# One ring of weight pieces across stage ends, and the first top-16 pass inside the key-score stages, in a hybrid encoder step

## The chip, the cores and the metric

One core of a Trainium2 chip runs the whole program. The metric is the device time of an execution in microseconds.

## What is computed

One inference step of a two-layer encoder, for 256 prompt tokens and 128 sample tokens (8 streams of 16), so three tiles of 128 tokens, width 1024, f32. Each layer has a mixer (layer 0: RWKV-7; layer 1: differential attention) and an expert mixer:

```python
q = (xr @ w_query).reshape(n, PEER_HEADS, 2, PEER_DHALF)
s = jnp.einsum('nhcd,ckd->nhck', q, sub_keys)            # 8 heads x 2 halves x 128 keys
s1, i1 = lax.top_k(s[:, :, 0], 16); s2, i2 = lax.top_k(s[:, :, 1], 16)
cand_s = (s1[..., :, None] + s2[..., None, :]).reshape(n, 8, 256)
top_s, top_pos = lax.top_k(cand_s, 16)                   # 128 experts a token
h = gelu(einsum('nhkd,nd->nhk', expert_u[eidx], xr))
out = einsum('nhk,nhkd->nd', softmax(top_s) * h, expert_v[eidx])
x = layer_norm(alpha * x + out)
```

Sample tokens attend over 512 cached positions of their stream (K and V, 32 MB together) beside their own.

## The kernel before

The first 700 us (projections of layer 0, its recurrence for the prompt tiles) are not touched. After that runs the **expert flow**: for each of six units (three tiles by two layers; `u` 0 to 5) 128 rows of `peer_uv` a token, one gather for each of 128 slots, [128, 2048] f32 (1 MB). Two gathers are a **turn**, 64 turns a unit, 384 in all. `Flow` (L1160) spreads each turn over the engines: POOL issues the gathers (L1357) into ring `fl_pairs` of 8 places, with 2 more (`fl_more`) except for rows 68 to 223; DVE makes the dots (L1283) and multiplies by the gate (L1273); ACT does gelu (L1309) and a scaled diagonal (L1303); PE sums with it into PSUM (L1330), which frees the place.

All else is written as **stages**, each a block that all engines leave together, with **ticks**: after each piece of its own work every engine calls `flow.vector`, `.scalar`, `.tensor` or `.gpsimd` for that tick. `flow.plan(ticks, last, ...)` spreads the turns up to number `last` evenly over the ticks; dots come first, mixes a tick later, PE's sums two ticks later. So the table of `last` numbers in `experts_and_attention` (L3082) sets how much of the flow each stage carries. `lead` ticks of flow (3) stand ahead of a stage's own products while its weights load.

The stages of a tile of layer 1 (`attention_tile`, L2951), in order: `ffn_norm` (L1567); `turn_features` (L1624); `attention_projections` (L1674), K, V and Q from 12 pieces of 1 MB in a ring of three; `turn_features` of K and Q; `prompt_attention` or, for the sample tile, `sample_attention` (L1901) with 16 K and 16 V pieces, rings of three and of two, issued in turn by SP with waits between (`Cache`, L1881); `head_norm`; `project_tile` (L2189), four pieces in places of their own, all asked for at the stage's start; `turn_features`; `key_scores` (L2259), eight pieces in a ring of two, 16 products of 8 matmuls, then 16 score products in four groups. The mixing tile of layer 0 ends with the same last three stages after its own. Each ring belongs to its stage, so its first load is issued when the stage begins. DMAs by SP are asked for in the order of its program.

The choice of experts from scores (`Choice.steps`, L1108) is DVE work: top 16 of 128 for 16 half heads (max8, index, replace, max8, index), 256 sums a head into `ch_cand`, top 16 of those, then the indices by compare and reduce. It is cut into units; `side` units are spread over the ticks of the three stages after key scores, and end at tick `end`. Then `turn_rows_out` and `turn_rows_in` on POOL store and reload the indices in the flow's layout at the ticks in `turn`; only then can that unit's rows be gathered. For the last unit a plain flow stage, `run_flow` with 24 ticks, carries this.

```python
p = min(range(self.KEPT if g in self.NARROW else self.PLACES), key=lambda i: -1 if last[i] is None else last[i])
...
due = self.first + (self.last - self.first) * n // self.ticks
...
advance(self.part, self.side * n // self.ticks - self.side * (n - 1) // self.ticks)
```

## Time and profile before

| | |
|---|---|
| median of 3 runs | 3353.61 us (3338.91 to 3354.03) |
| the profiled execution | 3348.66 us, its span 3346.9 |
| PE busy | 2178.8 us, 65% of the span |
| DVE busy | 1772.7 us, 53% |
| ACT, POOL busy | 675.0 us, 1055.2 us |
| HBM read | 1001.23 MB, 305 GB/s over the span |
| gathers | 768, of 1 MB |

Engines' rows are times that the engine works; waits, branches and DMA issue are not in them. A window row gives a stretch of the span, then for PE, weight load, DVE, ACT and POOL the busy us and instructions, then the granted clock of TensorE, the DMA engines' mean busy share and GB/s. The windows used are cut where the engines leave a stage.

### The profile page before, as it was taken

The numbers are of one execution on the slowest core, as the hardware profiler recorded it, in microseconds if no ns is written. First come the engines' busy times: TensorE is split into PE (matmuls) and PEld (weight loads), VectorE is DVE, ScalarE is ACT, GpSimd is POOL, SyncE is SP. The second block draws the span as 40 slices with busy tenths as digits, with TensorE's granted clock in tenths as the row PEclk, the third lists the DMA queues.
The fourth block names the chain that finished last, engine by engine and source line by source line (L and its number), as shares of the span: only waits on it lengthen the run. The fifth ranks groups of instructions, "written<-read, shape, count | busy, mean of one in ns | idle before, by whom it ended". The sixth has DMA issues, their size and how long they took to land. (4 is left out here: it accounts for less than half of the span.)

```text
span 3346.9 us, 33701 instructions
## 1 busy us (share of the span) xinstructions
PE 2178.8 (65%) x11881; PEld 1175.2 (35%) x11881; DVE 1772.7 (53%) x4126; ACT 675.0 (20%) x1932; POOL 1055.2 (32%) x990
## 2 busy tenths in 40 slices
PE   6949486755558677667566575665846676645555
PEld 3428375452225344253223322233213434312221
DVE  2143433167856575518653676544753353775555
ACT  1022121011122231111411114211113321121111
POOL 0013031014435354211332333423331232444442
PEclk9979687788779898778787887778877887877887
DMA  5220201459999999978799998999998889989998
GB/s 179 94 113 1 76 1 55 166 156 420 401 352 362 394 366 380 359 273 345 282 381 382 365 407 312 386 400 359 423 376 357 333 356 381 370 325 421 420 420 337
DMA packets 154118, 1028.10 MB, mean 307 GB/s; under 512 B 18016, under 2 KB 19216, under 8 KB 37728
## 3 DMA queue, kind: packets, MB, share of 16 engines
q0 software_dynamic: 117024, 825.84, 62.2%
q1 hardware_dynamic: 36928, 200.10, 15.1%
q8 instruction: 97, 1.59, 0.2%
q14 instruction: 69, 0.57, 0.0%
HBM read 1001.23 MB, written 18.39 MB: 305 GB/s over the span
## 5 line engine op out<-in xcount | busy, mean ns | idle before, releaser
L1330 PE MATMUL fl_acc<-fl_pairs,fl_diag 128*64 128x512 f32 x2584 | 855.8, 762 | 545.9 <-ACT fl_diag L1303 519.2
L1357 POOL DMA_INDIRECT fl_pairs<-in_peer_uv,fl_row_at x646 | 733.4, 1135 | 1329.1 <-PE fl_acc L1330 1216.5
L1283 DVE CUSTOM_DVE_ANT_0 fl_pairs<-fl_pairs,fl_rows 128x1024 f32<-128x1024 f32 x646 | 780.8, 1233 | 303.1 <-DMA fl_pairs<-in_peer_uv,fl_row_at 299.6
L1330 PEld LDWEIGHTS fl_acc<-fl_pairs,fl_diag 128*64 128x64 f32 x2584 | 299.2, 166 | 983.5 <-issue 927.1
L1303 ACT ACTIVATE fl_diag<-constants_sb,fl_mix 128x64 f32<-128x64 f32 x768 | 224.7, 341 | 377.5 <-DVE fl_mix L1273 366.6
L1309 ACT ACTIVATE fl_acts<-fl_dots 128x2 f32<-128x2 f32 x384 | 78.1, 204 | 1063.2 <-DVE fl_dots L1283 1054.3
L1273 DVE TENSOR_TENSOR fl_mix<-fl_row_gate,fl_acts 128x2 f32<-128x2 f32 x384 | 72.7, 190 | 301.6 <-ACT fl_acts L1309 256.8
L1357 POOL DMA_INDIRECT fl_more<-in_peer_uv,fl_row_at x122 | 142.2, 1166 | 255.3 <-PE fl_acc L1330 233.9
L1330 PE MATMUL fl_acc<-fl_more,fl_diag 128*64 128x512 f32 x488 | 164.5, 775 | 85.4 <-ACT fl_diag L1303 83.6
L1283 DVE CUSTOM_DVE_ANT_0 fl_more<-fl_more,fl_rows 128x1024 f32<-128x1024 f32 x122 | 146.3, 1222 | 45.7 <-DMA fl_more<-in_peer_uv,fl_row_at 45.3
L1713 PE MATMUL aacc<-aw_ring,at_xT 128*128 128x512 f32 x288 | 137.2, 622 | 11.8 <-DMA aw_ring<-in_kvq_by_pair 11.8
L1429 PE MATMUL pbank_late<-at_yT,wq_late 128*128 128x128 f32 x768 | 105.1, 298 | 53.7 <-DMA wq_late<-in_query_by_head 53.7
L284 PE MATMUL acc<-w_ring,mixed 128*128 128x512 f32 x288 | 125.9, 599 | 10.0 <-issue 9.1
L1429 PEld LDWEIGHTS pbank_late<-at_yT,wq_late 128*128 128x128 f32 x768 | 97.6, 208 | 78.6 <-DMA wq_late<-in_query_by_head 61.0
L1330 PEld LDWEIGHTS fl_acc<-fl_more,fl_diag 128*64 128x64 f32 x488 | 57.6, 168 | 172.8 <-issue 166.1
L1713 PEld LDWEIGHTS aacc<-aw_ring,at_xT 128*128 128x128 f32 x288 | 53.5, 196 | 99.0 <-issue 78.1
L348 DVE SCALAR_TENSOR_TENSOR mixed<-dxT,mu_cols,xT 128x384 f32<-128x384 f32 x48 | 25.8, 612 | 114.4 <-PEq L293 114.4
L284 PEld LDWEIGHTS acc<-w_ring,mixed 128*128 128x128 f32 x288 | 55.1, 192 | 80.1 <-issue 80.1
L1454 ACT COPY qT_late<-pbank_late 128x128 f32<-128x128 f32 x64 | 17.0, 266 | 241.6 <-PE pbank_late L1429 232.4
L1283 DVE DVE_READ_ACCUMULATOR2_ANT fl_dots<- 128x1 f32 x768 | 63.3, 82 | 0.0
L721 DVE TENSOR_TENSOR x<-bank,x 128x512 f32<-128x512 f32 x32 | 22.1, 692 | 77.1 <-PE bank L579 77.1
L1383 POOL DMA_DIRECT2D fl_rows<-x_tok x24 | 12.8, 554 | 154.3 <-POOLq L1468 153.0
(506 smaller groups left out, 2994.3 us busy)
## 6 DMA issues: line engine op xcount, KB each, us to landing
aw_ring<-in_kvq_by_pair SPq DMA_DIRECT2D x36, 1024.0 KB
wq_late<-in_query_by_head SPq DMA_DIRECT2D x32, 1024.0 KB
cache_k<-in_past_k SPq DMA_DIRECT2D x16, 1024.0 KB
cache_v<-in_past_v SPq DMA_DIRECT2D x16, 1024.0 KB, 10.3
w_ring<-in_rwkv_w_rkv SPq DMA_DIRECT2D x24, 512.0 KB, 3.2
pt_w<-in_out_by_pair SPq DMA_DIRECT2D x12, 1024.0 KB, 22.3
fl_pairs<-in_peer_uv,fl_row_at POOLq DMA_INDIRECT x646
fl_pairs<-in_query_by_head SPq DMA_DIRECT2D x8, 1024.0 KB, 8.0
```

Source lines behind the costliest of these rows:

```text
L284: mm = pe.matmul(acc[:, 2 * t + h, :], xm[:, k, t * P:(t + 1) * P], w_ring[:, n % RING, h * HALF:(h + 1) * HALF], start=(k == 0), stop=(k ...
L348: ins = dve.scalar_tensor_tensor(mixed[:, j % 2, k, :], dxT[:, k, :], mu_cols[:, i * KD + k:i * KD + k + 1], xT[:, k, 0:TOK], ALU.mult, AL ...
L721: dve.tensor_tensor(x[:, g % 2, (i + 1) % 2], quad(bank[4 + i % 2], P), x[:, g % 2, i % 2], ALU.add).then_inc(*x_done.by())
L1273: dve.tensor_tensor(self.mix[:, u % 2, q, :], self.row_gate[:, u % TILES, :, q], self.acts[:, u % 2, q, :], ALU.mult).then_inc(*self.mix_d ...
L1283: dve.tensor_tensor_reduce(pair, pair, self.rows[:, u % 2, j, :], 1.0, 0.0, ALU.mult, ALU.add, self.dots[:, u % 2, q, j:j + 1]).then_inc(* ...
L1303: act.activation(self.diag[:, self.diagged % self.DIAGS, j, :], self.core.const("fold_ident"), ACT.Copy, scale=self.mix[:, u % 2, q, j:j + ...
L1309: act.activation(self.acts[:, u % 2, q, :], self.dots[:, u % 2, q, :], ACT.Gelu).then_inc(*self.gelu_done.by())
L1330: mm = pe.matmul(self.acc[j * FOLD:(j + 1) * FOLD, half, :], self.diag[:, self.summed % self.DIAGS, j, :], self.pair(g)[:, D + half * HALF ...
L1357: pool.indirect_dma_start(self.pair(g), None, self.io["peer_uv"], bass.IndirectOffsetOnAxis(ap=self.row_at[:, u % TILES, j, q:q + 1], axis ...
L1429: mm = pe.matmul(self.bank[m % 3][:, 0:self.width], self.wq[:, m // 2 % self.ring, k, (m % 2) * P:(m % 2 + 1) * P], self.xT[:, k, self.row ...
L1454: act.copy(self.qT[:, m, :], self.bank[m % 3][:, 0:self.width]).then_inc(*self.q_done.by())
L1713: mm = pe.matmul(acc[:, 2 * i + h, :], xT[:, k, :], ring[:, n // 2 % RING, n % 2, h * HALF:(h + 1) * HALF], start=(k == 0), stop=(k == KD ...
```

## The change

Every weight and cache load of the second part, 116 pieces of 1 MB, is one sequence (`Pieces`) through one ring of four places (a fifth for the cache blocks). Each stage's SP program asks for pieces up to four past its own last one, each as soon as the piece before it in its place is used. The three lead ticks go from projections, output projections and key scores. `KeyScores` stays for the first two units; the four late ones use `LateScores`: score products follow each four half heads, and DVE does that group's first top-16 pass within the stage. What is left of the choice (`rest`) runs in the stages after, with the sums laid over the scores' tile. The table of turns is new.

```diff
-        self.cand = sb("cand", [P, PH, PTOP * PTOP])
...
+    def best_of(self, dve, place, group):
+        heads = range(group * self.GROUP, (group + 1) * self.GROUP)
+        yield from top16(dve, self.flow.choose_steps, self.flow.passed, [self.best[:, m, :] for m in heads],
+                         [self.best_at[:, m, :] for m in heads], [self.scores[:, place, m, :] for m in heads])
...
+        for group in range(self.HC // self.GROUP):
+            yield from self.best_of(dve, place, group)
+        yield from self.rest(dve, u, place)
...
+        cand = self.scores[:, place].rearrange("p (h c) k -> p h (c k)", c=2)
...
-                self.part = self.choice.steps(dve, self.u, self.place)
+                self.part = self.choice.rest(dve, self.u, self.place)
...
+    PLACES, MORE = 4, 1
...
+        self.expect("mix", [flat(io["mix_by_pair"][k]) for k in range(KD // 2)])
+        self.expect("query0", [flat(io["query_by_head"][0, i]) for i in range(PH)])
+        for t in range(TILES):
+            self.expect(f"kvq{t}", [flat(io["kvq_by_pair"][n]) for n in range(3 * KD // 2)])
+            if t == 2:
+                past = {n: [flat(io[f"past_{n}"][i // 2, i % 2]) for i in range(2 * DEC_BATCH)] for n in "kv"}
+                order = [("k", 0), ("k", 1)]
+                for b in range(1, DEC_BATCH):
+                    order += [("k", 2 * b), ("k", 2 * b + 1), ("v", 2 * b - 2), ("v", 2 * b - 1)]
+                order += [("v", 2 * DEC_BATCH - 2), ("v", 2 * DEC_BATCH - 1)]
+                start = len(self.sources)
+                self.past = {key: start + j for j, key in enumerate(order)}
+                self.expect("past", [past[n][i] for n, i in order])
+                wide = range(start + self.PLACES, len(self.sources))
+            self.expect(f"out{t}", [flat(io["out_by_pair"][k]) for k in range(KD // 2)])
+            self.expect(f"query1{t}", [flat(io["query_by_head"][1, i]) for i in range(PH)])
+        last, used = [None] * (self.PLACES + self.MORE), [0] * (self.PLACES + self.MORE)
+        self.place_of, self.before, self.count = [], [], []
+        for n in range(len(self.sources)):
+            p = min(range(self.PLACES + self.MORE if n in wide else self.PLACES), key=lambda i: -1 if last[i] is None else last[i])
+            used[p] += 1
+            self.place_of.append(p)
+            self.before.append(last[p])
+            self.count.append(used[p])
+            last[p] = n
...
+    def load(self, sp, upto):
+        for n in range(self.loaded, min(upto, len(self.sources))):
+            if self.before[n] is not None:
+                sp.wait_ge(*self.freed[self.before[n]])
+            sp.dma_start(self.tile(n), self.sources[n]).then_inc(*self.came[self.place_of[n]].by(16))
+        self.loaded = max(self.loaded, min(upto, len(self.sources)))
...
+            pieces.freed[first + i] = self.q_psum.at(2 * i + 2)
+    def loads(self, sp):
+        sp.dma_start(self.keysT[:], self.io["keys_turned"][self.layer]).then_inc(*self.keys_in.by(16))
+        self.pieces.load(sp, self.first + PH + self.pieces.PLACES)
...
+        def scores(q):
+            pe.wait_ge(*self.q_done.at(4 * q + 4))
+            if q == 0:
+                pe.wait_ge(*self.keys_in.at(16))
+            for m in range(4 * q, 4 * q + 4):
+                mm = pe.matmul(self.bank[3 + q % 3][:, (m % 4) * P:(m % 4 + 1) * P], self.qT[:, m, :], self.keysT[:, m % 2, :])
+            mm.then_inc(*self.s_psum.by())
+        for m in range(self.HC):
+            n = self.first + m // 2
+            if m % 2 == 0:
+                pe.wait_ge(*self.pieces.ready(n))
+            if m >= 3:
+                pe.wait_ge(*self.q_done.at(m - 2))
+            w = self.pieces.tile(n).rearrange("p (k n) -> p k n", k=KD)
+            for k in range(KD):
+                mm = pe.matmul(self.bank[m % 3][:, 0:P], w[:, k, (m % 2) * P:(m % 2 + 1) * P], self.xT[:, k, :], start=(k == 0), stop=(k == KD - 1))
+            mm.then_inc(*self.q_psum.by())
+            if m % 4 == 0 and m > 0:
+                scores(m // 4 - 1)
+            self.flow.tensor(pe, m + 1)
+        pe.wait_ge(*self.s_done.at(1))
+        scores(self.HC // 4 - 1)
...
+    def best(self, dve):
+        group = None
+        for n in range(1, self.ticks + 1):
+            if n % 4 == 2 and 2 < n <= self.HC + 2:
+                q = n // 4 - 1
+                dve.wait_ge(*self.s_done.at(q + 1))
+                group = self.choice.best_of(dve, 0, q)
+            if group is not None:
+                advance(group, 5)
+            if n % 4 == 1 or n == self.ticks:
+                drain(group if group is not None else ())
+            self.flow.vector(dve, n)
...
+            pieces.freed[first + n] = aw_used.at(2 * n + 2)
...
-                for n in range(3 * KD // 2):
-                    if n >= RING:
-                        sp.wait_ge(*aw_used.at(2 * (n - RING + 1)))
-                    sp.dma_start(ring[:, n % RING], io["kvq_by_pair"][n]).then_inc(*aw_in[n % RING].by(16))
+                pieces.load(sp, first + 3 * KD // 2 + pieces.PLACES)
...
-    PLACES = {"k": 3, "v": 2}
...
+            pieces.freed[pieces.past["k", i]] = sc.at(3 * (i // 2) + 2 + i % 2)
+            pieces.freed[pieces.past["v", i]] = v_used.at(i + 1)
...
+                pieces.load(sp, pieces.first["past"] + 2 * HALVES * DEC_BATCH + pieces.PLACES)
...
+        for k in range(KD // 2):
+            pieces.freed[first + k] = w_used.at(k + 1)
...
-                for k in range(KD // 2):
-                    sp.dma_start(wt[:, 2 * k:2 * k + 2, :], weight[k]).then_inc(*w_in[k].by(16))
                 sp.dma_start(g[:], io["ln_mix_g"][layer:layer + 1, :].broadcast_to([P, D])).then_inc(*vec_in.by(16))
                 sp.dma_start(b[:], io["ln_mix_b"][layer:layer + 1, :].broadcast_to([P, D])).then_inc(*vec_in.by(16))
+                pieces.load(sp, first + KD // 2 + pieces.PLACES)
...
+            turn_features(core, flow, [([gated[:]], mixT)], f"mt_g{t}", last, store=lambda sp: pieces.load(sp, pieces.PLACES), **events)
...
-    mixing_tile(core, io, flow, 2, None, [
-        (43, {}), (63, {}), (71, {}), (76, {}), (96, {}), (104, {}), (105, {}), (110, {}), (111, {}), (116, {})])
+    later = ExitStack()
+    pieces = mixing_tile(core, io, flow, 2, None, later, [
+        (43, {}), (63, {}), (71, {}), (76, {}), (96, {}), (104, {}), (105, {}), (110, {}), (111, {}), (120, {})])
-        attention_tile(core, io, flow, 0, neg_lam, kT, v_tok, [
-            (118, dict(rows=((2, 1),), choose=2, side=20)), (119, dict(side=20)), (125, dict(side=110, end=23, turn=((2, 26, 29),))), (130, {}), (138, {}), (142, {}), (152, {}), (154, {}), (166, {})])
-        attention_tile(core, io, flow, 1, neg_lam, kT, v_tok, [
-            (169, dict(rows=((3, 1),), choose=3, side=15)), (170, dict(side=15)), (185, dict(side=120, end=24, turn=((3, 27, 29),))), (190, {}), (202, {}),
-            (206, {}), (215, {}), (217, {}), (229, {})])
-    attention_tile(core, io, flow, 2, neg_lam, None, None, [
-        (232, dict(rows=((4, 1),), choose=4, side=15)), (234, dict(side=15)), (250, dict(side=120, end=24, turn=((4, 27, 29),))), (255, {}), (273, {}),
-        (276, {}), (284, {}), (286, {}), (296, {})])
-    run_flow(core, flow, 24, 318, choose=5, side=160, end=20, rows=((5, 1),), turn=((5, 23, 0),))
+        attention_tile(core, io, flow, pieces, 0, neg_lam, kT, v_tok, [
+            (122, dict(rows=((2, 1),), choose=2, side=20)), (123, dict(side=20)), (134, dict(side=50, end=9, turn=((2, 11, 13),))), (140, {}),
+            (149, {}), (153, {}), (159, {}), (162, {}), (176, {})])
+        attention_tile(core, io, flow, pieces, 1, neg_lam, kT, v_tok, [
+            (180, dict(rows=((3, 1),), choose=3, side=20)), (182, dict(side=20)), (196, dict(side=50, end=9, turn=((3, 11, 13),))), (202, {}),
+            (213, {}), (217, {}), (223, {}), (226, {}), (240, {})])
+    attention_tile(core, io, flow, pieces, 2, neg_lam, None, None, [
+        (244, dict(rows=((4, 1),), choose=4, side=20)), (246, dict(side=20)), (260, dict(side=50, end=9, turn=((4, 11, 13),))), (266, {}),
+        (296, {}), (299, {}), (304, {}), (306, {}), (313, {})])
+    run_flow(core, flow, 8, 318, choose=5, side=70, end=6, rows=((5, 1),), turn=((5, 8, 0),))
+    later.close()
```

SP, from the output projection of the mixing tile to the first K, V, Q projections (`pt_w`, `wq_late`, `aw_ring` were the stages' own rings, `pc_ring` is the common one). Before:

```order
L2211 DMA pt_w<-in_mix_by_pair 128x2048 x4
L2212 DMA pt_g<-in_ln_mix_g 128x1024
L2213 DMA pt_b<-in_ln_mix_b 128x1024
L2207 UNCONDITIONAL_BRANCH
L2265 UNCONDITIONAL_BRANCH
L1413 DMA keysT_late<-in_keys_turned 128x256
L1417 DMA wq_late<-in_query_by_head 128x2048 x8
L2264 UNCONDITIONAL_BRANCH
L1582 UNCONDITIONAL_BRANCH
L1584 DMA fn_g<-in_ln_ffn_g 128x1024
L1585 DMA fn_b<-in_ln_ffn_b 128x1024
```

Now:

```order
L2321 DMA pt_g<-in_ln_mix_g 128x1024
L2322 DMA pt_b<-in_ln_mix_b 128x1024
L1459 DMA pc_ring<-in_query_by_head 128x2048 x4
L2318 UNCONDITIONAL_BRANCH
L2374 UNCONDITIONAL_BRANCH
L1486 DMA keysT_late<-in_keys_turned 128x256
L1459 DMA pc_ring<-in_query_by_head 128x2048 x4
L1459 DMA pc_ring<-in_kvq_by_pair 128x2048 x4
L2373 UNCONDITIONAL_BRANCH
L1726 UNCONDITIONAL_BRANCH
L1728 DMA fn_g<-in_ln_ffn_g 128x1024
L1729 DMA fn_b<-in_ln_ffn_b 128x1024
```

Half of a stage's pieces are asked for in the stage before, and the vectors of `ffn_norm` stand behind four pieces of the next projections.

DVE, in the key scores of attention tile 0. Before, turns alone:

```order
L1273 TENSOR_TENSOR fl_mix<-fl_row_gate,fl_acts 128x2
L1283 ISA fl_pairs,fl_dots<-fl_pairs,fl_rows 128x1024
L1283 ISA fl_dots 128x1
L1283 ISA fl_pairs,fl_dots<-fl_pairs,fl_rows 128x1024
L1283 ISA fl_dots 128x1
```

Now, with the pass over one group of four half heads between them:

```order
L1062 MAX ch_best<-ch_scores 128x8 x4
L1068 MAX_INDEX ch_best_at<-ch_best,ch_scores 128x8
L1288 TENSOR_TENSOR fl_mix<-fl_row_gate,fl_acts 128x2
L1068 MAX_INDEX ch_best_at<-ch_best,ch_scores 128x8 x3
L1071 MATCH_REPLACE ch_scores<-ch_best,ch_scores 128x128 x2
L1298 ISA fl_pairs,fl_dots<-fl_pairs,fl_rows 128x1024
L1298 ISA fl_dots 128x1
L1298 ISA fl_pairs,fl_dots<-fl_pairs,fl_rows 128x1024
L1298 ISA fl_dots 128x1
L1071 MATCH_REPLACE ch_scores<-ch_best,ch_scores 128x128 x2
L1077 MAX ch_best<-ch_scores 128x8 x3
```

The mixes and dots of a tick stand behind a wait for scores, and behind the group's units. The same pass stood at the head of the choice in the stages after.

## Rows read from the trace of the kernel before

**Rows 1.** The page, slices: busy tenths of the DMA engines, and GB/s.
```profile
DMA  5220201459999999978799998999998889989998
GB/s 179 94 113 1 76 1 55 166 156 420 401 352 362 394 366 380 359 273 345 282 381 382 365 407 312 386 400 359 423 376 357 333 356 381 370 325 421 420 420 337
```

**Rows 2.** Windows A to F: length, busy us by engine, PEclk, DMA share, GB/s.
```profile
1358.30:1491.50 133.20, 95.11 (x440) 58.07 (x440) 38.16 (x77) 19.65 (x67) 29.67 (x28) 0.80 0.80 313
1491.50:1869.90 378.40, 246.03 (x900) 113.57 (x900) 223.45 (x579) 88.04 (x266) 115.76 (x108) 0.81 0.88 348
1869.90:2302.80 432.90, 283.33 (x1036) 127.63 (x1036) 261.25 (x644) 105.68 (x309) 145.43 (x137) 0.81 0.94 374
2302.80:2863.30 560.50, 368.14 (x2004) 184.81 (x2004) 281.38 (x721) 119.60 (x354) 161.51 (x148) 0.80 0.91 366
2863.30:3015.90 152.60, 77.56 (x208) 30.27 (x208) 122.21 (x348) 26.98 (x85) 68.10 (x63) 0.73 0.91 357
3015.90:3343.90 328.00, 183.48 (x504) 72.97 (x504) 175.28 (x329) 54.82 (x194) 133.67 (x118) 0.79 0.97 401
```

**Rows 3.** Windows, plain flow stages of 8 and of 50 turns.
```profile
3015.90:3056.40 40.50, 22.96 (x64) 8.74 (x64) 21.08 (x40) 6.32 (x24) 18.91 (x17) 0.79 1.01 420
3082.40:3331.10 248.70, 146.19 (x400) 57.87 (x400) 131.28 (x250) 39.48 (x150) 107.16 (x95) 0.80 1.00 412
```

**Rows 4.** Windows of single stages: one of A, three of B, four each of C, D.
```profile
1419.10:1491.50 72.40, 52.89 (x328) 42.63 (x328) 12.25 (x25) 9.53 (x35) 9.46 (x10) 0.79 0.70 272
1528.50:1599.30 70.80, 58.68 (x144) 22.71 (x144) 60.52 (x187) 10.50 (x27) 16.68 (x17) 0.89 0.82 335
1703.90:1766.30 62.40, 43.95 (x120) 16.41 (x120) 31.95 (x60) 11.14 (x35) 23.22 (x22) 0.83 1.01 421
1783.90:1869.90 86.00, 63.41 (x376) 43.16 (x376) 29.50 (x60) 13.82 (x56) 25.21 (x22) 0.88 0.92 367
1908.30:2015.50 107.20, 78.37 (x208) 28.93 (x208) 84.99 (x252) 17.54 (x54) 32.45 (x31) 0.87 0.99 407
2050.10:2118.10 68.00, 41.30 (x160) 16.74 (x160) 52.22 (x123) 42.52 (x100) 21.76 (x20) 0.78 0.78 297
2143.20:2201.90 58.70, 40.76 (x112) 15.59 (x112) 29.60 (x55) 10.36 (x32) 21.77 (x21) 0.85 1.01 421
2218.30:2302.80 84.50, 63.81 (x376) 43.48 (x376) 29.41 (x60) 13.80 (x56) 25.64 (x22) 0.86 0.94 378
2344.90:2459.60 114.70, 81.91 (x216) 30.02 (x216) 87.81 (x258) 18.45 (x57) 37.66 (x32) 0.84 0.97 401
2494.00:2695.00 201.00, 130.13 (x1144) 75.37 (x1144) 77.47 (x211) 58.10 (x151) 40.87 (x36) 0.79 0.88 354
2714.80:2767.70 52.90, 34.85 (x96) 12.31 (x96) 26.64 (x49) 9.08 (x27) 19.53 (x18) 0.82 1.00 413
2784.60:2863.30 78.70, 61.32 (x368) 44.04 (x368) 24.51 (x50) 12.45 (x50) 20.85 (x19) 0.85 0.89 354
```

**Rows 5.** Waits from 1358 to 3344: us in total, times, longest us.
```profile
PE pbank_late L1429 <- DMA wq_late<-in_query_by_head: 70.9, 17, 8.4
...
PE sa_b L1976 <- DMA cache_k<-in_past_k: 52.6, 8, 8.8
...
DVE fl_ffn L1616 <- DMA fn_b<-in_ln_ffn_b: 34.8, 4, 10.7
```

**Rows 6.** Waits of the first late key-score stage, 1419.1 to 1491.5.
```profile
DVE fl_mix L1273 <- ACT fl_acts L1309: 55.2, 4, 17.0
...
PE pbank_late L1429 <- DMA wq_late<-in_query_by_head: 17.1, 3, 7.0
```

**Rows 7.** Window of the last choice: DVE's work on `ch_scores`, then on `ch_cand`.
```profile
2863.30:2982.60 119.30, 20.12 (x128) 0.00 (x0) 0.74 0.94 372
2863.30:2982.60 119.30, 31.57 (x71) 0.74 0.94 372
```

**Rows 8.** Timeline of POOL at the end of that choice.
```profile
2994.43 1.24 POOL L1374 DMA_DIRECT2D fl_row_at<-turn_at  x2 [11.40 <-DMA turn_gate<-fl_gate]
```

209 lines of the change are left out of this document (105 added, 104 removed).

## The prediction

> **What bounds the kernel now.** I read the page's slices first: from slice 10 on the DMA engines are busy mostly eight or nine tenths and move mostly 350 to 420 GB/s, and where nothing disturbs them they stay at 420 [rows 1]. No compute engine is near that in this part. So the part after the first projection stages is bound by transfers, with gaps. How large the gaps are is read from windows cut at the stage ends. I call **lost time** of a window its length times (1 - GB/s / 420): the time by which it is longer than its bytes need. Five stretches [rows 2] lose 33.9 us (A, end of mixing), 64.9 (B, attention tile 0), 47.4 (C, tile 1), 72.1 (D, tile 2) and 22.9 (E, last choice of experts), 241 us together; the sixth (F) is not touched and loses 14.8.
>
> What a turn of the expert flow costs comes from the plain flow stages [rows 3]: 8 turns in 40.5 us at 420 GB/s, so 2.1 MB and 5.0 us a turn where transfers bound it; 50 turns hold PE 146.2 us and DVE 131.3, so 2.9 and 2.6 us a turn. A turn placed in a stage that waits for something else costs about 2.9 us there and takes away 5.0 elsewhere.
>
> Then single stages [rows 4]. The key-score stages and the one of projections lose time, the output projections (421 GB/s) none. The chain of waits says why: PE stands 70.9 us for query weights over the four late key-score stages, 17.1 of them in the first [rows 6], and 52.6 us for K blocks in attention over the cache [rows 5]; weight rings of two places, and a K and a V ring that share one SP queue, are too short, and every stage begins with its first weight still to come.
>
> **The change part by part.** Bytes and pieces stay the same: 116 weight or cache pieces of 1 MB and 768 gathers. What changes is when they are asked for and how many turns each stage carries.
>
> *The piece ring.* At each stage's end four pieces of the next user are in flight or landed. That takes away PE's waits: some 18 us in each key-score stage and 53 us in attention over the cache. Cover: none needed at stage starts, so the three lead ticks of flow go. Price: four more pieces fall into A (4.2 MB, 10 us) and four fewer into D; SP's FFN-norm vectors now stand behind a prefetched piece. DVE already waits for them 34.8 us in four places [rows 5]. One piece alone is 2.5 us at 420 GB/s and 5 us beside the gathers, three stages: 8 to 15 us, I take **8** because the mean of the present waits says that part overlaps. The trace cannot show less than nothing here.
>
> The Trainium skill (DMA: Bandwidth & Descriptors, section Queues, rings and completion order) says that on each DMA engine descriptors are consumed in ring order, so the vectors behind a piece pay for it. No row here shows that order itself; by the rule the charge would be the full 15, and the time 7 us longer.
>
> *The turns*, by the schedule table. A: 12 to 16. B: 50 to 56. C: 63 to 64. D: 67 to 73. E: 26 to 9. For each stage I take the larger of its bytes at 420 GB/s and its old time less the removed wait plus 2.9 us per added turn, and a few us where both are close.
> - A: 133.2 us at 313 GB/s is 41.7 MB; with four turns and four pieces 54.3 MB, 129.3 us. Engines: 133.2 - 18 + 11.6 = 127. Both are close, I take **139** (10 lost). That is +6 for 20 us of turns and 10 us of pieces.
> - B [rows 2, 4]: projections from 6 to 11 turns with 12 pieces are 35.7 MB, 85 us floor, 88 taken for 70.8 (+17). Output projection 10 to 6 turns, 17.8 MB, 44 for 62.4 (-18). Key scores 12 to 14 turns, 37.8 MB is 90 us, 92 for 86 (+6). The other six stages carry three more turns net: +8. **391** for 378.4.
> - C: projections 15 to 14 turns, 101 for 107.2; output projection 9 to 6, 44 for 58.7; key scores 92 for 84.5; prompt attention 12 to 11, 65 for 68; the rest +7. **424** for 432.9.
> - D: attention over the cache from 18 to 30 turns: 62.9 MB of rows and 32 pieces, 96 MB, 229 us floor. Engines: 201 - 53 + 12 x 2.9 = 183. So it is bound by transfers, 237 for 201 (+36). Projections 101 for 114.7, output projection 42 for 52.9, key scores 10 to 7 turns 62 for 78.7, rest +4. **557** for 560.5.
> - E: the choice of tile 5. DVE spends 20.1 us on the first pass over the scores and 31.6 us on what follows on the candidates [rows 7], some 34 with the small steps. The first pass moves into key scores, under PE. What stays is 34 + 5 x 2.6 = 47 us in a stage with five turns, 50 with waits, then the norm stage, 33. POOL sits 11.4 us there for its own store of the indices before it may load them [rows 8], as before. **83** for 152.6.
>
> Sum: 139 + 391 + 424 + 557 + 83 = 1594 against 1657.6, so -64, and +8 for the vectors: **-56**. Of the expected 241 us of lost time 185 stay: latency chains of norms, turns of features and prompt attention, which no ring helps. In E more is lost than before (38 for 23), since turns that covered the choice are gone; late next is DVE there.
>
> *Moved first pass in key scores.* DVE waits at ticks 6, 10, 14 and 18 for a group of scores. Behind it stand mix and dots of that tick, which PE wants two ticks later. A tick is 3.7 us (86.0 us by 23 ticks [rows 4]); the group's 5 us of DVE work is spread over four. DVE has 14 x 2.6 + 20 = 57 us of work in 92. I cost it at nothing; bounds are zero and the price under the slower rival.
>
> *Other edits.* The candidates now lie over the scores, same operations, nothing. The next tile's indices are known at tick 13 of the projections and not at the end: in B rows of tile 2 run out while pieces flow, so 3 us of lost time in my 88; from 0 to 15 us, I take the low end since eight pieces (8.4 MB, 20 us) fill that hole.
>
> The profiled execution is 3348.66 us, 1.8 over its span, and 5 under the median of the three runs (3353.61). 3348.7 - 56 = 3293; with a little of that 5, **3295 us**. A measurement of this kernel tells some 0.5% (17 us) from no change.
>
> **The rivals.**
> - *More goes* (3225 us): more even turns also fill features and norm stages, half of the 139 us left in A to D goes. For: output projections at 421 GB/s lose nothing, so a full queue closes all. Against: those with 1 to 5 turns end on chains.
> - *Waits only change names* (3335): weights come early but rows then come late, and PE waits for rows as it did for K blocks. Of the 56 some 16 stay. For: DVE waits for rows in all stages already; against: where the queue is full that wait is the floor itself.
> - *Transfers at their ceiling* (3349): if the mean rate of these stretches (366 GB/s over A to F by [rows 2]) were the most there is, nothing could go. Rows at 420 [rows 3] over 40 us speak against it. The Trainium skill (DMA: Bandwidth & Descriptors, section Specifications) gives about 358 GB/s as HBM limit per core and 435 for the fabric; by the first there is no gain and the time is 3349, by the rows the forecast. The trace disagrees with the first.
> - *Hidden anyway* (3343): weights waited for are covered by lead ticks of flow today and by nothing then, so the prefetch buys back what the leads gave: only 8 us of the sum stay.
> - *Slower: DVE held in key scores* (3395). In `best` DVE waits for PE's product of head 4q and ACT's copy. If that comes more than one tick after DVE is there, mixes and dots come late by one to two ticks, and PE stands for each of 4 groups in 4 stages: 16 x 1.5 x 4.2 = 100 us. For: in the first key-score stage DVE already waits for ACT 55.2 us in 4 places [rows 6]. Against: that is DVE being early; PE's two ticks (8 us) are longer than mix, dots and copy. It decides once PE's waits for the diagonals exceed 4 us each there.
>
> **How the numbers follow.** Forecast 0.50, more goes 0.15, names 0.17, ceiling 0.03, hidden 0.07, slower 0.08. Half of the third lies past the bound of 3337, so faster 0.74, same 0.18, slower 0.08. The range 3220 to 3350 leaves out the slower case and the low end of the second. The forecast's own range is 3265 to 3320.
>
> **What would show it.** Key scores without waits for weights and at over 400 GB/s; attention over the cache about 237 us at over 400; output projections near 44; the plain flow stage after the last key scores about 50 with DVE busy nearly throughout; lost time over A to E near 185. It is wrong if attention over the cache is above 255, if PE waits for diagonals in key scores, or if projections in B exceed 100 for want of indices.

## The result, and the profile after

The changed kernel takes 3232.9 us (median of 4 runs, 3230.2 to 3235.8) against 3352.2 for the kernel before in the same comparison (4 runs): ratio 0.965, 95% interval 0.963 to 0.968. That is faster, with 119 us gone where 57 were forecast (3295 us). The time lies within the range of 3220 to 3350, and below the forecast's own range of 3265 to 3320.

The page of the changed kernel, its two slice rows that answer to [rows 1]:

```profile
DMA  5230200367998999999899999999999999969998
GB/s 169 94 137 1 79 1 18 130 214 307 420 390 318 371 366 370 373 418 351 352 402 394 419 383 399 390 375 419 395 384 421 420 420 401 387 243 421 420 420 339
```

Between slices 21 and 35 none is below 375 GB/s now; before, seven of these fifteen were. Slice 36, at 243, holds the end of the last choice.

Windows of the changed kernel, cut at the stage ends: first the six stretches A to F (as [rows 2]), then single stages: key scores and B's projections, B's output projection and key scores, attention over the cache, D's output projection and key scores, and the two stages of E (as [rows 4]). The columns are those of [rows 2].

```profile
1366.30:1488.70 122.40, 95.16 (x472) 55.32 (x472) 67.99 (x225) 22.80 (x79) 36.17 (x35) 0.85 1.01 415
1488.70:1870.70 382.00, 254.05 (x948) 114.41 (x948) 240.97 (x609) 95.58 (x286) 127.25 (x122) 0.82 0.95 382
1870.70:2288.00 417.30, 286.19 (x1044) 126.22 (x1044) 266.16 (x649) 106.51 (x312) 151.48 (x138) 0.81 0.98 394
2288.00:2827.10 539.10, 376.28 (x2052) 195.70 (x2052) 299.54 (x751) 122.58 (x371) 172.05 (x158) 0.85 0.99 403
2827.10:2900.80 73.70, 30.56 (x72) 12.33 (x72) 61.99 (x135) 13.57 (x34) 30.00 (x30) 0.65 0.64 226
2900.80:3227.80 327.00, 181.75 (x504) 73.08 (x504) 175.13 (x329) 54.82 (x195) 131.59 (x117) 0.81 0.97 403
...
1424.50:1488.70 64.20, 57.45 (x360) 41.85 (x360) 42.00 (x173) 12.68 (x47) 17.40 (x17) 0.87 1.01 419
1527.50:1616.80 89.30, 70.71 (x184) 26.10 (x184) 46.89 (x84) 15.33 (x43) 24.02 (x27) 0.86 0.83 327
1723.40:1764.20 40.80, 29.18 (x88) 9.62 (x88) 21.78 (x40) 7.99 (x23) 16.15 (x15) 0.85 1.00 408
1782.20:1870.70 88.50, 65.64 (x392) 44.53 (x392) 55.51 (x198) 15.81 (x62) 29.67 (x28) 0.92 1.01 419
2468.70:2696.60 227.90, 152.79 (x1232) 91.18 (x1232) 108.05 (x270) 63.64 (x184) 63.33 (x60) 0.87 1.01 420
2719.20:2754.80 35.60, 27.99 (x80) 9.54 (x80) 19.00 (x34) 6.72 (x18) 12.81 (x13) 0.91 1.01 422
2769.10:2827.10 58.00, 51.69 (x344) 40.41 (x344) 37.28 (x163) 11.20 (x41) 13.24 (x12) 0.91 0.93 373
2827.10:2876.60 49.50, 17.44 (x40) 6.71 (x40) 45.53 (x106) 6.83 (x18) 14.99 (x14) 0.63 0.58 194
2876.60:2900.80 24.20, 13.12 (x32) 5.62 (x32) 16.46 (x29) 6.75 (x16) 15.01 (x16) 0.69 0.79 292
```

A to E add up to 1534.5 us, against 1657.6 before and 1594 in the forecast: 123 us gone. F is 1 us shorter. The part ahead of A, which the change does not touch, was 8 us longer in this execution (A begins at 1366.3, at 1358.3 before), so the spans differ by 116. Lost time, by the prediction's definition, is now 1.5 us (A), 34.6 (B), 25.8 (C), 21.8 (D) and 34.0 (E): 118 us, where it was 241 and where 185 were expected.

What DVE and POOL waited for in the changed kernel, 1366 to 3228 us (us in total, times, longest; against [rows 5, 6]):

```profile
PE fl_acc L1345 <- ACT fl_diag L1318: 426.3, 145, 16.4
DVE fl_pairs L1298 <- DMA fl_pairs<-in_peer_uv,fl_row_at: 383.5, 232, 14.4
...
POOL fl_row_at L1389 <- DMA turn_gate<-fl_gate: 39.3, 3, 18.2
POOL turn_at L1379 <- DVEq L1172: 33.0, 2, 17.6
...
DVE ch_best L1062 <- ACT ch_scores L1519: 15.9, 8, 2.9
```

No row has PE waiting for `pc_ring`: the 70.9 us for query weights and the 52.6 us for K blocks [rows 5] are gone. DVE waits for gathered rows instead (238.0 us in 161 places before), which is what a stage filled with bytes looks like from the compute side. DVE's wait for the first score pass is 15.9 us in eight places. PE does wait for the diagonals in the four late key-score stages: 42.0 us in 18 places, the longest 4.4, 5.6, 5.6 and 4.5 us in A to D, where before it was 3.9 us once in each.

### The profile page after: what moved, and what is told of

Its sections match the earlier page's. It is cut to its first block and busy times, and to the rows that moved or that the text cites. A ratio compares the mean times of both kernels' runs of the same rounds, so it can differ in the third digit from the quotient of the medians.

```text
span 3230.8 us, 33794 instructions
## 1 busy us (share of the span) xinstructions
PE 2154.2 (67%) x11881; PEld 1166.3 (36%) x11881; DVE 1785.3 (55%) x4126; ACT 676.0 (21%) x1934; POOL 1049.0 (32%) x990
## 5 line engine op out<-in xcount | busy, mean ns | idle before, releaser
L1345 PE MATMUL fl_acc<-fl_pairs,fl_diag 128*64 128x512 f32 x2584 | 842.5, 753 | 526.0 <-ACT fl_diag L1318 494.2
L1851 PE MATMUL aacc<-pc_ring,at_xT 128*128 128x512 f32 x288 | 141.1, 635 | 16.0 <-PEq L1778 16.0
L1506 PEld LDWEIGHTS lbank_late<-at_yT,pc_ring 128*128 128x128 f32 x768 | 92.0, 199 | 27.7 <-issue 27.7
L1506 PE MATMUL lbank_late<-at_yT,pc_ring 128*128 128x128 f32 x768 | 97.2, 286 | 4.1 <-PEq L1778 3.7
L1851 PEld LDWEIGHTS aacc<-pc_ring,at_xT 128*128 128x128 f32 x288 | 54.8, 201 | 103.1 <-issue 103.1
L348 DVE SCALAR_TENSOR_TENSOR mixed<-dxT,mu_cols,xT 128x384 f32<-128x384 f32 x48 | 25.8, 613 | 115.1 <-PEq L293 115.1
L1398 POOL DMA_DIRECT2D fl_rows<-x_tok x24 | 12.8, 558 | 160.0 <-POOLq L1612 152.6
L2112 PE MATMUL sa_b<-pc_ring,sa_pT 128*32 128x128 f32 x384 | 45.1, 320 | 23.1 <-ACT sa_pT L2142 23.1
```

Of the source, the lines that this page charges most:

```text
L348: ins = dve.scalar_tensor_tensor(mixed[:, j % 2, k, :], dxT[:, k, :], mu_cols[:, i * KD + k:i * KD + k + 1], xT[:, k, 0:TOK], ALU.mult, AL ...
L1345: mm = pe.matmul(self.acc[j * FOLD:(j + 1) * FOLD, half, :], self.diag[:, self.summed % self.DIAGS, j, :], self.pair(g)[:, D + half * HALF ...
L1506: mm = pe.matmul(self.bank[m % 3][:, 0:P], w[:, k, (m % 2) * P:(m % 2 + 1) * P], self.xT[:, k, :], start=(k == 0), stop=(k == KD - 1))
L1851: mm = pe.matmul(acc[:, 2 * i + h, :], xT[:, k, :], pieces.tile(first + n // 2)[:, n % 2 * D + h * HALF:n % 2 * D + (h + 1) * HALF], start ...
L2112: mm = pe.matmul(o_bank[rows, g * P:(g + 1) * P], pT[:, g, j, rows], v, start=(j == 0), stop=(j == KT), tile_position=(0, h * HR))
```

## The experiments

All ratios are against the kernel before, run in the same comparison; one thousandth is 3.3 us. Three questions were open: which of the three parts (ring, table of turns, early first pass) carries the gain; whether inside the ring it is the common depth or the reach over stage ends; and what the time still lost would give back.

**Old table of turns.** The changed kernel with the turns at the stage ends of the kernel before (in the stages of a choice the short `rest` stays, and the last unit's indices are reloaded within its stage):

```diff
-            (43, {}), ... (110, {}), (111, {}), (120, {})
+            (43, {}), ... (110, {}), (111, {}), (116, {})
-            (122, dict(rows=((2, 1),), choose=2, side=20)), (123, dict(side=20)), (134, ...
+            (118, dict(rows=((2, 1),), choose=2, side=20)), (119, dict(side=20)), (125, ...
...
-        (296, {}), (299, {}), (304, {}), (306, {}), (313, {})])
-    run_flow(core, flow, 8, 318, choose=5, side=70, end=6, rows=((5, 1),), turn=((5, 8, 0),))
+        (273, {}), (276, {}), (284, {}), (286, {}), (296, {})])
+    run_flow(core, flow, 24, 318, choose=5, side=210, end=8, rows=((5, 1),), turn=((5, 11, 13),))
```

> The changed kernel with the old table of turns (116, 166, 229, 296 at the ends of A to D; the last choice again in a plain flow stage of 22 turns). Theory 'table and ring need each other' (the ring only takes PE's waits away, turns must be moved in to use the bytes' time): attention over the cache falls from 201 us to about 172 (its bytes' floor), key scores by 5 to 18 us each, in all some 75 us less than before: 3275 us, so 40 more than the changed kernel. Rival 'the ring alone': within 10 us of the changed kernel (3233). Rival 'the table alone': 3340 or more.

Measured: 3230.5 us, 0.963 (0.962 to 0.965), so the rival "the ring alone" held and the table gives nothing in all; turns taken out of attention over the cache come back in the last choice one for one. Windows of this kernel, attention over the cache and the last choice:

```profile
2441.30:2601.90 160.60, 127.06 (x1144) 75.12 (x1144) 77.00 (x211) 57.86 (x152) 40.07 (x36) 0.86 1.01 420
2755.90:2879.10 123.20, 65.45 (x176) 26.02 (x176) 89.33 (x191) 20.14 (x69) 58.95 (x55) 0.72 0.92 359
```

With the old 18 turns the cache stage runs at 420 GB/s too (201 us at 354 before, [rows 4]). It did not need twelve more turns to be full; it needed its blocks in time.

**No reach over stage ends.** The changed kernel, every stage asking for its own pieces only:

```diff
-        self.pieces.load(sp, self.first + PH + self.pieces.PLACES)
+        self.pieces.load(sp, self.first + PH)
...
-            turn_features(core, flow, [([gated[:]], mixT)], f"mt_g{t}", last, store=lambda sp: pieces.load(sp, pieces.PLACES), **events)
+            turn_features(core, flow, [([gated[:]], mixT)], f"mt_g{t}", last, **events)
```

> The changed kernel whose ring of four never reaches over a stage's end: each stage asks for its own pieces only. Theory 'cross-stage': eleven users (mix, four key scores, three projections, cache blocks, output projections) start with an empty ring, PE stands 5 to 8 us at each start for its first piece, and the DMA engines have only gathers over feature turns, norms and prompt attention, where they lost little in the changed kernel: 40 to 70 us slower than 3233. Rival 'depth': four places within a stage are what matters, under 12 us slower.

Measured: 3283.1 us, 0.979 (0.977 to 0.981), some 46 to 50 us slower than the change, as the first theory had it. PE's waits for pieces in this kernel:

```profile
PE lbank_late L1506 <- DMA pc_ring<-in_query_by_head: 51.4, 4, 15.1
...
PE pt_acc L2336 <- DMA pc_ring<-in_out_by_pair: 44.6, 3, 15.4
...
PE aacc L1851 <- DMA pc_ring<-in_kvq_by_pair: 38.8, 3, 13.3
```

The first piece of each of these stages keeps PE 13 to 15 us on average, not the 5 to 8 that I counted for a piece beside gathers. The mixing weights are waited for once, 16.3 us. These 151 us of waits cost 50 us of time.

**First pass back in the choice.** The changed kernel, with the pass over the scores in the stages after, and more steps a tick there:

```diff
-                self.part = self.choice.rest(dve, self.u, self.place)
+                self.part = self.choice.steps(dve, self.u, self.place)
...
-                part.best(dve)
+                for n in range(1, flow.ticks + 1):
+                    flow.vector(dve, n)
```

> The changed kernel with the first top-16 pass back in the stages after key scores (norm, feature turn, first nine ticks of projections; run_flow for the last unit). Theory: DVE has 20 us more between key scores and the indices, four times. In B rows of unit 2 then come 20 us later and nothing covers it, in E the same; in C and D half of it: 50 to 60 us slower than 3233, key-score stages unchanged within 2 us. Rival 'DVE has room': under 15 us slower.

Measured: 3296.8 us, 0.984 (0.982 to 0.986), some 62 to 64 us slower than the change. Windows, B's projections and the last choice:

```profile
1531.40:1631.90 100.50, 73.47 (x184) 28.78 (x184) 58.45 (x136) 15.22 (x43) 24.94 (x27) 0.86 0.75 295
2867.40:2939.20 71.80, 15.90 (x40) 6.32 (x40) 65.85 (x234) 6.83 (x18) 11.90 (x15) 0.60 0.49 164
```

The new table cannot do without the early pass: indices of the next tile come late while few turns are left to cover it. This alone does not say that the pass is worth 64 us, since its own table is the one that needs it; the ring alone answers that below. The key-score stages did not all stay as they were: without the pass D's takes 50.8 us for 58.0 and A's 60.6 for 64.2.

**Turns moved in the kernel before.** No ring, no early pass; attention over the cache takes 30 turns, and the last choice 8 fewer:

```diff
-    (255, {}), (273, {}), (276, {}), (284, {}), (286, {}), (296, {})
+    (255, {}), (285, {}), (288, {}), (293, {}), (295, {}), (302, {})
```

> The kernel before (old rings) with twelve turns moved into attention over the cache (18 to 30), and the following stages of D as in the new table (3, 5, 2, 7), so 16 turns and not 22 in the last choice's stage. Theory 'bytes fill it even with the old rings': attention over the cache takes about 240 us, PE's 53 us of waits for K do not add to it, and the whole is 10 to 25 us faster than before (3335). Rival 'old rings hold it back': 255 us or more there, and no gain (3350 or more).

Measured: 3329.2 us, 0.993 (0.990 to 0.995), a gain of 24 us, as the first theory had it. Window and wait of attention over the cache:

```profile
2500.20:2725.10 224.90, 150.38 (x1232) 81.56 (x1232) 105.86 (x270) 65.84 (x185) 70.72 (x58) 0.83 1.00 410
```

```profile
PE sa_b L1976 <- DMA cache_k<-in_past_k: 54.1, 8, 8.7
```

PE waits for K blocks as long as before (54.1 us, [rows 5] 52.6), yet the stage moves 410 GB/s: in a stage filled with turns these waits cost at most the 5 us that it still loses. So table and ring are two ways to the same idle time of this stage (201.0 us at 354 GB/s are 32 us lost, [rows 4]), and they do not add up there.

**The ring alone.** The changed kernel with the old table and the first pass in the old place, so the edits of the first and the third experiment, and the steps and ticks of the choices near those of before. Two small parts of the change stay in it and were not tried apart: the lead ticks are gone, and the score products follow each four half heads.

```diff
-            (119, dict(side=20)), (125, dict(side=50, end=9, turn=((2, 11, 13),)))
+            (119, dict(side=20)), (125, dict(side=110, end=20, turn=((2, 23, 26),)))
...
-    run_flow(core, flow, 24, 318, choose=5, side=210, end=8, rows=((5, 1),), turn=((5, 11, 13),))
+    run_flow(core, flow, 24, 318, choose=5, side=160, end=20, rows=((5, 1),), turn=((5, 23, 0),))
```

> The ring of pieces across stage ends with nothing else of the change: old table, first top-16 pass back in the stages after key scores, indices at the end of the projections as before. Theory 'two halves that add' (ring worth the query and K waits and the transfers over norms and feature turns; first pass worth 20 us of DVE before each unit's indices): 3280 to 3295 us, so the ring gives some 65 of the 120 and the early pass the rest. Rival 'the ring is nearly all': under 3255. Rival 'the pass is nearly all': over 3320.

Measured: 3222.3 us, 0.968 (0.965 to 0.970), so the rival "the ring is nearly all" held; once more beside the others (below) 0.968 (0.966 to 0.971). Its windows A to E, then the key scores of A, B, C, attention over the cache and the key scores of D:

```profile
1346.10:1453.20 107.10, 85.67 (x440) 52.52 (x440) 38.33 (x77) 19.84 (x67) 26.63 (x27) 0.85 1.00 410
1453.20:1819.60 366.40, 238.51 (x900) 109.81 (x900) 225.17 (x579) 88.76 (x266) 120.11 (x110) 0.82 0.91 361
1819.60:2238.30 418.70, 275.21 (x1036) 122.28 (x1036) 262.98 (x644) 106.33 (x309) 146.13 (x136) 0.82 0.96 386
2238.30:2729.60 491.30, 352.30 (x2004) 180.07 (x2004) 281.63 (x721) 119.77 (x353) 160.38 (x145) 0.85 1.00 408
2729.60:2887.10 157.50, 78.48 (x208) 32.02 (x208) 123.39 (x348) 26.98 (x85) 71.05 (x65) 0.73 0.92 362
...
1405.90:1453.20 47.30, 45.44 (x328) 38.07 (x328) 12.25 (x25) 9.72 (x35) 7.57 (x9) 0.94 1.00 406
1745.30:1819.60 74.30, 59.61 (x376) 41.47 (x376) 30.57 (x60) 14.52 (x56) 26.55 (x22) 0.87 1.01 419
2165.40:2238.30 72.90, 58.65 (x376) 41.28 (x376) 30.38 (x60) 14.42 (x56) 26.17 (x22) 0.90 1.01 420
2421.50:2579.90 158.40, 123.59 (x1144) 75.55 (x1144) 77.24 (x211) 57.84 (x151) 39.42 (x36) 0.90 1.01 415
2673.50:2729.60 56.10, 54.65 (x368) 41.16 (x368) 24.51 (x50) 12.86 (x51) 20.02 (x17) 0.96 0.99 398
```

With the same turns as [rows 2] (x77, x900, x1036, x2004: the counts of DVE and PE are those of before) the five stretches take 1541.0 us for 1657.6: 117 less. Four key-score stages and the cache stage are shorter by 114 of them: 72.4 to 47.3, 86.0 to 74.3, 84.5 to 72.9, 78.7 to 56.1 and 201.0 to 158.4. So the ring alone brings some 108 us (0.968 of 3350) of the 119. [rows 5] leaves out that PE also waited for other pieces before, 1358 to 3344 us:

```profile
PE aacc L1713 <- DMA aw_ring<-in_kvq_by_pair: 11.8, 4, 5.1
PE pt_acc L2228 <- DMA pt_w<-in_out_by_pair: 6.0, 2, 5.5
PE pt_acc L2228 <- DMA pt_w<-in_mix_by_pair: 4.6, 1, 4.6
```

With the 123.5 us of [rows 5] that is 146 us of PE's waits for pieces. The ring alone has 14.2 left (11.6 and 2.6, both for K blocks), so 132 us of waits went for 117 us of time.

**Its depth alone.** The same kernel with the edit of the second experiment (`PLACES` taken off in every stage's load): four common places, but every stage starts with its first piece.

> The ring alone (old table, old choice) and without reaching over stage ends: four places within each stage, each stage starting empty, no lead ticks. Theory 'half depth, half ends' (the ring's 108 us are PE's 124 us of waits, of which those for K blocks and most of those for queries come in mid-stage): 0.981 to 0.985, since the start of ten stages costs some 5 us each as it did with the new table (50 us). Rival 'all of it is the ends': 0.995 or more, since what depth gives the missing lead ticks take.

Measured: 3301.4 us, 0.987 (0.985 to 0.990), between the two, nearer to the first. Depth gives 43 us, the reach over stage ends the other 65. The cache stage is 168.0 us here at 420 GB/s, so it profits from depth. PE waits 60.7 us for query weights, 45.1 for output weights, 38.7 for projections, 16.3 for the mixing weights and 20.6 for K blocks, 181 together. That is 167 more than the 14.2 us of the ring alone, and they are worth 66 us of time (0.020 of 3350). (Output projections and projections waited only 6.0 and 11.8 us before, with lead ticks of flow ahead of their first piece. The reach pays for taking them out.)

**The choice of tile 2 pushed forward.** The changed kernel, to close the hole in B's rows:

```diff
-            (122, dict(rows=((2, 1),), choose=2, side=20)), (123, dict(side=20)), (134, dict(side=50, end=9, turn=((2, 11, 13),)))
+            (122, dict(rows=((2, 1),), choose=2, side=24)), (123, dict(side=24)), (134, dict(side=104, end=2, turn=((2, 4, 6),)))
```

> The changed kernel with unit 2's choice pushed forward (24 units of it in each of norm and feature turn, the rest in the first two ticks of the projections, store and reload of the indices at ticks 4 and 6 instead of 11 and 13). Theory 'B's projections lose 20 us because rows run out before the indices': lost time there falls from 20 to about 8, the whole by 10 to 14 us to 3220. Rival 'norm and feature turn grow by as much, since DVE is late there': within 4 us of the changed kernel.

Measured: 3230.5 us, 0.969 (0.967 to 0.971): no gain, as the rival had it. Projections fall from 89.3 to 82.6 us, and the turning of features before them grows from 13.5 to 24.0 us at 239 GB/s, now that DVE has the choice there (busy 21.6 us).

**Five turns later.** The changed kernel, 25 turns in the cache stage and 10 in the stage of the last choice:

```diff
-        (296, {}), (299, {}), (304, {}), (306, {}), (313, {})])
-    run_flow(core, flow, 8, 318, choose=5, side=70, end=6, rows=((5, 1),), turn=((5, 8, 0),))
+        (291, {}), (294, {}), (299, {}), (301, {}), (308, {})])
+    run_flow(core, flow, 12, 318, choose=5, side=72, end=10, rows=((5, 1),), turn=((5, 12, 0),))
```

> The changed kernel with five turns moved from attention over the cache (30 to 25) to the stage of the last choice (5 to 10, in 12 ticks). Theory 'E loses 36 us because only five turns cover DVE's 34 us and the reload': cache attention is 25 us shorter, E longer by 5 x 2.6 = 13 us, the whole 12 us faster: 3221. Rival 'gathers of those turns stand behind the choice in time too': no gain, within 4 us.

Measured: 3207.9 us, 0.963 (0.961 to 0.965). Windows, attention over the cache and the last choice:

```profile
2448.40:2651.20 202.80, 142.13 (x1200) 87.34 (x1200) 95.69 (x246) 60.29 (x171) 52.52 (x51) 0.88 1.01 420
2786.00:2845.80 59.80, 28.08 (x80) 11.16 (x80) 57.18 (x131) 10.66 (x33) 25.43 (x24) 0.71 0.84 312
```

Five turns more cost the last choice 10 us (49.5 to 59.8), and their 25 us are saved in the cache stage (227.9 to 202.8); the norm stage after the choice takes 3 more (24.2 to 27.6). The whole is only 0.2% lower, where 12 us (0.4%) were expected. This and the edit before it together:

> Both of the two before. If each acts at its own place they add: 22 to 26 us faster than the changed kernel, 3209. If one only moves the other's lost time, no more than the better of the two.

Measured: 3216.4 us, 0.965 (0.963 to 0.967), not better than the later turns alone.

**The changed kernel again, and the choice at the front.** In a third comparison:

> The changed kernel itself, on the same chip as the three beside it, as their measure. All theories: 0.965 of before.

Measured: 3228.9 us, 0.965 (0.962 to 0.967). Then with 22 turns in the cache stage and 13 in the last choice, whose indices come at ticks 11 and 13 of 16:

```diff
-        (296, {}), (299, {}), (304, {}), (306, {}), (313, {})])
-    run_flow(core, flow, 8, 318, choose=5, side=70, end=6, rows=((5, 1),), turn=((5, 8, 0),))
+        (288, {}), (291, {}), (296, {}), (298, {}), (305, {})])
+    run_flow(core, flow, 16, 318, choose=5, side=128, end=9, rows=((5, 1),), turn=((5, 11, 13),))
```

> Eight turns moved from cache attention (30 to 22) to the last choice's stage (13 turns in 16 ticks), the choice pushed to its front and the indices stored and loaded at ticks 11 and 13. Theory: E loses only what stands before the reload, 15 us and not 36, and D nothing more, so 20 us under the changed kernel, 0.959. Rival 'five turns were enough' (the version with five moved): 0.963 again.

Measured: 3224.7 us, 0.964 (0.961 to 0.966), not the 0.959 of the theory. And on top of it two turns fewer in A:

```diff
-        (111, {}), (120, {})])
+        (111, {}), (118, {})])
...
-            (122, dict(rows=((2, 1),), choose=2, side=20)), (123, dict(side=20)), (134, ...
+            (120, dict(rows=((2, 1),), choose=2, side=20)), (121, dict(side=20)), (132, ...
```

> The same, and two turns fewer in A (118 at its end), with B's norm, turn and projections also two lower, so two more turns of known rows are left while unit 2's indices are made. Theory: B's projections lose 10 us and not 20, but key scores of A lose 3: 5 us better than the kernel beside it. Rival 'rows only wait elsewhere': within 3 us of it.

Measured: 3216.3 us, 0.962 (0.960 to 0.965). The intervals of the two overlap, so this decides nothing.

**Four of these kernels again, side by side**, to see what early pass and table add to the ring, and whether a version beats the change: ring alone; ring and early pass with the old table; later turns; the front-loaded one.

> The ring alone again, beside the next. Theory 'the rest gives little': 0.966 to 0.968.

> Ring and early pass on the old table again. Theory 'DVE's 20 us before each unit's indices were mostly hidden': within 6 us of the ring alone. Rival 'the early pass gives 13 us': 0.963 to 0.964 beside 0.967.

> The changed kernel with five turns moved to the last choice's stage, again: 0.963 if it held on the first chip, against 0.9645 of the changed kernel.

> The best table so far again: 0.961 to 0.963, so 8 to 15 us under the ring alone.

| version | us | ratio | interval |
|---|---|---|---|
| ring alone | 3240.8 | 0.968 | 0.966 to 0.971 |
| ring and early pass, old table | 3232.9 | 0.966 | 0.963 to 0.968 |
| later turns | 3221.8 | 0.963 | 0.960 to 0.965 |
| front-loaded choice, A with two turns fewer | 3218.6 | 0.963 | 0.960 to 0.965 |

The early pass with the old table stands 8 us below the ring alone, with intervals that overlap, and the change itself (0.965) is no better than that. The last two versions have twice given 0.962 to 0.963. They probably beat the change by some 0.2 to 0.3%, though the intervals overlap.

The windows of these kernels say why the early pass gives so little: it costs time where it runs. With the old table and the pass, the key scores of A and of D (without it: 47.30 and 56.10 us above):

```profile
1425.50:1481.70 56.20, 47.53 (x328) 39.09 (x328) 32.37 (x153) 10.00 (x35) 9.34 (x9) 0.86 0.92 367
2693.40:2756.10 62.70, 56.39 (x368) 40.90 (x368) 44.37 (x178) 13.26 (x50) 19.08 (x19) 0.95 1.00 406
```

That is 9 and 7 us more, and 8 and 7 in the pair run again; in B and C, at 403 to 420 GB/s, it costs nothing. It gives back 10 us in B's projections, 7 in C's turning of K and Q and 7 in the two stages of E, and 11, 7 and 8 in the second pair.

## Why the prediction was right in sign and half in size

**The ring was summed wrong.** The step that failed is "for each stage I take the larger of its bytes at 420 GB/s and its old time less the removed wait plus 2.9 us per added turn, and a few us where both are close". It came out too long wherever pieces were loaded. The removed waits were named (18 us a key-score stage, 53 us in the cache stage; 123.5 us in [rows 5]), but I never wrote down what the ring gives with the old table, which is the sum 1657.6 - 123.5 = 1534. The runs show 1541 for it, in part by luck: the sum leaves out 22.4 us of waits that also went, and stage by stage it does not fit (key scores of A 25 us shorter for 17 us of waits, of B 12 for 20, the cache stage 43 for 53). Then the forecast credited the new turns as a second source, with a margin on every stage near its floor. The margins were not there. The forecast of the stretches was too long by 17 us in A, 9 in B, 7 in C, 18 in D and 9 in E, and by the 8 for the vectors. By its own items (those of D add up to 559, not to the 557 written), A and the stages with pieces in B, C and D were 57 us too long, E's norm stage 9, and all other stages together 5 us too short. Stages near their floor run at the floor: key scores of A at 419 GB/s and A as a whole 122.4 us for 139; the cache stage 227.9 us at 420 for 237; key scores of B 88.5 at 419 for 92. In A the bytes were off too: 122.4 us at 415 GB/s are 50.8 MB, where I counted 54.3 from the turns.

**Chains that "no ring helps".** This step failed too: "Of the expected 241 us of lost time 185 stay: latency chains of norms, turns of features and prompt attention, which no ring helps". 118 stayed. Summed over those stages of A to D (norms, head norms, all turns of features, prompt attention), the lost time was 103 us before, 73 with the ring alone (73 when run again) and 41 in the changed kernel (41 again). Prompt attention of B before (C's is in [rows 4]), of B and C with the ring alone, and of B and C in the changed kernel:

```profile
1631.80:1676.50 44.70, 28.34 (x112) 11.15 (x112) 36.11 (x104) 31.47 (x85) 12.48 (x12) 0.81 0.75 290
...
1594.10:1638.70 44.60, 28.57 (x112) 11.18 (x112) 35.98 (x104) 31.45 (x84) 13.67 (x12) 0.81 0.75 288
1999.10:2066.50 67.40, 39.76 (x160) 16.26 (x160) 52.25 (x123) 42.42 (x99) 21.86 (x20) 0.80 0.77 297
...
1649.70:1697.30 47.60, 29.60 (x120) 11.38 (x120) 38.61 (x109) 34.87 (x89) 20.11 (x18) 0.82 0.97 388
2051.50:2113.20 61.70, 38.77 (x153) 15.73 (x152) 49.08 (x118) 40.71 (x95) 22.02 (x20) 0.83 0.91 354
```

The length of such a chain changes little, but bytes can move while it runs. The ring, whose pieces may land there, took 30 us of lost time from the norms and turns, and none from prompt attention. That is filled in every kernel with the new table (at most 7 us lost in B's, 10 in C's) and in none with the old (at least 13 and 15); as B's has one turn more and C's one fewer, it is not the number of turns in the stage alone, and what it is was not tried apart.

**The table of turns was taken for the main carrier.** In all it gives nothing. With the ring, old and new table give the same time (0.963 and 0.965); without it, moving twelve turns in D gives 24 us. The forecast's chain (ring removes waits, turns fill what is then free) is right in each stage, but a turn that fills one stage leaves another: E went from 152.6 to 73.7 us, and that is what A to D paid for by longer stages. Only lost time counts. Ring and early pass with the old table lose 62 us in the chain stages and 18 in E; with the new table it is 41 and 34.

**+8 for the vectors: not seen.** The wait of DVE for `fn_b` fell, from 34.8 us in four places [rows 5], in the changed kernel to:

```profile
  DMA fn_b<-in_ln_ffn_b: 3.6, 2
```

It was 8.8 us in three places when run again. The runs separate two things. With no piece of a later stage ahead of the vectors, the wait is 1.8 us in the changed kernel's table and 22.0 with the old table and choice; with such pieces it is 3.6 to 8.8, and 24.2 (19.1 again) in the ring alone. So standing behind prefetched pieces costs some 2 to 7 us with the new table, and nothing that stands out with the old. The fall itself comes with the early pass and the table (13.4 and 17.2 us with the pass and the old table, 9.4 with the new table and no pass), when DVE, it seems, comes later to these vectors. The rule of the Trainium skill that was weighed here (DMA: Bandwidth & Descriptors, section Queues, rings and completion order) may hold, and no run shows the order itself, but the price given by it, 15 us, and mine, 8, were both too high.

**B's indices: 3 us taken, 20 measured.** POOL's timeline in the changed kernel, projections of B:

```profile
1537.51 0.94 POOL L1372 DMA_INDIRECT fl_more<-in_peer_uv,fl_row_at  x1 [0.30 <-issue]
1556.01 0.61 POOL L1379 DMA_DIRECT2D turn_at<-fl_expert  x1 [17.55 <-DVEq L1172]
...
1561.56 1.23 POOL L1389 DMA_DIRECT2D fl_row_at<-turn_at  x2 [4.36 <-DMA turn_gate<-fl_gate]
...
1567.23 1.02 POOL L1372 DMA_INDIRECT fl_pairs<-in_peer_uv,fl_row_at  x1 [3.25 <-DMA fl_row_gate<-turn_gate]
```

For 30 us no gather is issued, and the stage moves 327 GB/s: it loses 19.8 us. The range given was 0 to 15, and I took the low end because pieces would fill the hole. They fill part of it only. That the stage took 89.3 us, where 88 were forecast, is luck: it moved 29.2 MB and not the 35.7 counted, and the 15 us less of transfer cover the hole.

**E was nearly right** (34.0 us lost, 38 expected): the choice took 49.5 us for 50, with DVE busy 45.5 of it. The norm stage after took 24.2 for 33. Output projections came out at 40.8 (B) and 35.6 (D) for 44 and 42.

**The rivals.** "More goes" at 3225 was nearest, and part of its mechanism did happen: A to D lose 84 us, where it halved the 139 of the forecast, and the new table filled the chain stages. But those turns were taken from E, where most of it was lost again (34 us for 18), so they were not what gave the time. "Waits only change names" fails: DVE's wait for rows grew from 238.0 to 383.5 us, but A to D move 382 to 415 GB/s meanwhile, against 313 to 374 [rows 2]. "Hidden anyway" left 8 us, and the ring alone gives 108. It is right in that lead ticks covered first pieces, for with depth alone they are waited for. For "slower" the deciding point was PE's wait for diagonals in key scores above 4 us each. Those waits came (42.0 us in 18 places, at most 5.6), without the price of 100 us: A to C stay at 419 GB/s. DVE's wait for scores is 15.9 us in eight places, at most 2.9 us. But the first pass under PE, costed at nothing, does cost 7 to 9 us each in the key scores of A and D at equal turns. The ceiling is refuted by 420 GB/s over 227.9 us; of the Trainium skill's two figures (same page, section Specifications) the trace stays with the one of 435 and not with the 358 per core.

**Open.** Whether early pass and table together give anything over the ring is below what these runs tell (0 to 0.5%). Of the 118 us still lost 20 lie in B's projections, 34 in E and 41 in the chain stages. For B's share the earlier choice gained nothing, and two turns fewer in A nothing clear; moving turns into E gave 0.2 to 0.3%.

## What to carry to other kernels

Sum what each part of a change gives alone before crediting a second part: two edits that both fill the same idle transfer time (a deeper prefetch, more work beside it) do not add up. Where transfers bound a kernel, cost everything in lost bytes per stage, and give a stage at its floor no margin; a wait of a compute engine is worth its length only where the transfers idle with it (132 us of removed waits were worth 117 here, 167 in the kernel with depth alone only 66, and 54 in a filled stage at most 5). A pass moved under an engine that isn't held up by transfers is not free: look at the stages that take it as well as at those that lose it. Let a ring of loads run over stage ends rather than covering each start with other work.

## What the runs showed that I had not expected

- A stage that asks for its first 1 MB piece at its own start, beside gathers under way, keeps PE 13 to 16 us on average until it has it (11 starts in each of two kernels), when the piece alone is 2.5 us of transfer. Four are asked for together there; how much of the wait that makes was not tried. In the ring alone a weight piece lands 9 to 12 us after it is asked for, in the median.
- Weight pieces on one queue and gathers on another share the engines without visible loss: 420 GB/s held over 227.9 us of mixed transfers, as over 40.5 us of gathers alone [rows 3].
- PE's granted clock in the key scores rose once PE no longer stood between pieces: from 0.79 to 0.94 in A and from 0.85 to 0.96 in D with the ring alone, that is nearer to the 2.4 GHz level (B and C: 0.88 to 0.87, 0.86 to 0.90). PE busy time in A fell from 52.9 to 45.4 us at the same 328 matmuls, which is part of why the ring gave more than the waits there (25.1 us for 17.1). With depth alone PE waits 14.2 us at the stage's start; from then on the clock is 0.98, and PE is busy 45.6 us too.
